# Banded attention with 512-key and 640-key query blocks in alternation

## The reference, cut to what matters

```python
def sliding_window_attention(q, k, v, k_c, v_c, sink):
    '''Banded attention |i - j| <= SWA_RADIUS plus all context keys, with sink logits.'''
    nb = seq // Q_BLOCK                       # 4 blocks of 128 queries
    band = np.abs(qoff[:, None] - koff[None, :]) <= SWA_RADIUS
    ...
    def block_step(j):
        start = j * Q_BLOCK
        ...
        kpos = start - SWA_RADIUS + jnp.arange(span)
        valid = band & ((kpos >= 0) & (kpos < seq))[None, :]
        mask = jnp.concatenate([valid, ctx_ok], axis=-1)
        return attend(q_j, jnp.concatenate([k_j, k_c], axis=1), jnp.concatenate([v_j, v_c], axis=1),
                      mask=mask, sink=sink)
```

## Time and profile before

| what | us |
|---|---|
| median of three runs | 3674.49 |
| lowest and highest of the three | 3672.79, 3674.63 |
| the profiled execution, its own time | 3677.19 |
| its span in the trace | 3675.4 |
| the banded attention, from its first scores to its last values | 3124.3 to 3263.2, 138.9 |

### The profile page before, as it was taken

One profiled execution on the slowest core, in us unless ns is written; L12 is line 12 of the kernel. 1 busy time (PEld: TensorE's weight loads), 2 busy tenths in 40 slices (PEclk: granted clock), 3 DMA queues, 4 the chain that ended last, 5 costly groups with the idle time before them and its releaser, 6 DMA issues.

```text
span 3675.4 us, 58161 instructions
## 1 busy us (share of the span) xinstructions
PE 3601.3 (98%) x19482; PEld 2948.1 (80%) x19482; DVE 2135.1 (58%) x3272; ACT 1832.1 (50%) x3517; POOL 1844.7 (50%) x1583
## 2 busy tenths in 40 slices
PE   9999999999999989999999999999999999999999
PEld 7877788888888767888888887788888997678887
DVE  6576742788635766427886664742236977743234
ACT  4565544434445664444444645843445653754343
POOL 4424673565544245735565763265564135145553
PEclk9999999999999999999999999999999999999999
DMA  4211241465322112414653422132223542012222
GB/s 145 94 64 41 75 144 63 154 192 190 105 92 86 64 41 84 145 59 163 192 188 109 143 89 90 59 104 97 97 92 119 175 166 81 2 58 86 97 97 86
DMA packets 106912, 388.58 MB, mean 106 GB/s; under 512 B 11856, under 2 KB 11984, under 8 KB 106320
## 3 DMA queue, kind: packets, MB, share of 16 engines
q1 hardware_dynamic: 87840, 318.81, 26.2%
q10 hardware_dynamic: 16416, 57.62, 4.7%
q0 software_dynamic: 2448, 9.43, 0.7%
HBM read 383.71 MB, written 2.10 MB: 105 GB/s over the span
## 4 chain that ended last, share of the span: by engine, by line
PE 74%; issue 13%; POOL 7%; DVE 4%; ACT 1%; ACTq 0%; POOLq 0%; DVEq 0%
PE ps L713 18%; PE ps L715 18%; PE ps L714 18%; POOL arena_parts L656 4%; PE ps L1207 2%; PE ps L2507 2%; PE ps L2530 2%; POOL arena_parts L666 1%; PE ps L2497 1%; PE ps L1226 1%; PE ps L1215 1%; POOL lines L440 1%; PE ps L1185 1%; PE ps L889 1%; PE ps L970 1%
## 5 line engine op out<-in xcount | busy, mean ns | idle before, releaser
L714 PE MATMUL ps<-arena_parts 128*128 128x512 f32 (+1 forms) x3148 | 1170.7, 372 | 0.0
L656 POOL TENSOR_TENSOR arena_parts<-ring,arena_parts 128x512 fp32r<-128x512 f32 x508 | 674.6, 1328 | 811.2 <-ACT arena_parts L633 809.1
L666 POOL TENSOR_TENSOR arena_parts<-ring,arena_parts 128x512 fp32r<-128x512 f32 x508 | 688.9, 1356 | 301.1 <-ACT arena_parts L642 300.0
L713 PE MATMUL ps<-h_parts,arena_parts 128*128 128x512 f32 x2080 | 814.5, 392 | 1.3 <-DVE arena_parts L563 1.2
L715 PE MATMUL ps<-h_parts,arena_parts 128*128 128x512 f32 x2080 | 809.4, 389 | 0.0
L1864 DVE SCALAR_TENSOR_TENSOR conv<-ps,cols,conv 128x511 f32<-128x511 f32 (+3 forms) x536 | 377.3, 705 | 536.9 <-ACT conv L1879 388.1
L714 PEld LDWEIGHTS ps<-arena_parts 128*128 128x128 f32 x3148 | 594.0, 189 | 104.4 <-issue 2.4
L633 ACT ACTIVATE arena_parts<-ring 128x512 fp32r<-128x512 f32 x574 | 360.2, 628 | 602.8 <-PE ps L715 570.8
L642 ACT ACTIVATE arena_parts<-ring 128x512 fp32r<-128x512 f32 x574 | 359.9, 627 | 596.2 <-PE ps L715 553.9
L713 PEld LDWEIGHTS ps<-h_parts,arena_parts 128*128 128x128 f32 x2080 | 390.5, 188 | 85.9 <-issue 3.3
L715 PEld LDWEIGHTS ps<-h_parts,arena_parts 128*128 128x128 f32 x2080 | 390.4, 188 | 81.0
(11 more groups left out here) (394 smaller groups left out, 6392.6 us busy)
## 6 DMA issues: line engine op xcount, KB each, us to landing
ring<-in_stream SPq DMA_DIRECT2D x606, 512.0 KB, 3.3
ctx<-in_mod ACTq DMA_DIRECT2D x48, 512.0 KB, 3.5
sq<-in_mod ACTq DMA_DIRECT2D x48, 512.0 KB, 3.4
sq<-in_bias POOLq DMA_DIRECT2D x8, 512.0 KB, 4.7
conv<-in_bias POOLq DMA_DIRECT2D x8, 512.0 KB, 4.5
arena<-in_mem ACTq DMA_DIRECT2D x2, 1024.0 KB, 5.7
out_y<-x ACTq DMA_DIRECT2D x8, 256.0 KB, 2.7
x<-in_x SPq DMA_DIRECT2D x4, 256.0 KB, 4.8
```

The source lines that it names most:

```text
L656: eng.tensor_tensor(side_of(lin, i, c, 0, to), side_of(lin, i, c, 0, raw), side_of(lin, i, c, 0, top), ALU.subtract)\
L666: eng.tensor_tensor(side_of(lin, i, c, 1, to), side_of(lin, i, c, 1, raw), side_of(lin, i, c, 1, top), ALU.subtract)\
L713: pe.matmul(out, w_h, x_h, start=start, stop=False)
L714: pe.matmul(out, w_h, x_r, start=False, stop=False)
```

## The change

The loop over a pair's four query blocks goes first, second, fourth, third. Nothing else is edited: masks, keys, values and the target columns of each block are worked out from its number b as before.

```diff
             for p in range(PAIRS):
                 kv = p // 2
-                for b in range(QB):
+                for b in (0, 1, 3, 2):
                     lo_b, hi_b = max(b - 1, 0), min(b + 2, QB)
```

## The result

| what | before | changed |
|---|---|---|
| median of the runs of one comparison, 20 each, us | 3672.67 | 3678.57 |
| lowest and highest | 3669.03, 3678.68 | 3675.51, 3684.31 |
| span of the profiled execution | 3675.4 | 3680.3 |
| the banded attention, first scores to last values | 3124.33 to 3263.20, 138.87 | 3125.56 to 3268.24, 142.68 |

The changed kernel takes 1.0015 times as long, interval 1.0009 to 1.0021, which is 5.5 us more, 3.3 to 7.7. That is inside the 0.2% that I had set as no change, and the time of 3678.57 is inside the range. The trace puts 3.8 us of it into the stage. Of the 4.9 us between the two spans, 1.2 had come up before the stage began, where the two kernels are the same; spans of one and the same kernel differ by more than that (3680.3 here, 3674.2 in the second trace of the changed kernel), so I compare stages and not spans.

A forecast was written before the change was run, and what follows sets the result against it. TensorE, busy 98% of the span, was taken as the bound, so only its waits could move the time. Steady pairs, first pair and last pair: 0.9 + 0.3 + 1.2 = +2.4 us, median 3676.9, range 3672.5 to 3681.0.

The forecast's parts named there:

- The wait at the boundary goes: Between pairs, the wait behind VectorE's L2189 would be hidden by an S at unit 5: 0.52 us a pair removed.
- 0.15 at each D even with VectorE free: At each D, TensorE's cover of 4.44 us against a chain of 4.59: a new wait of 0.15, 0.30 a pair.
- VectorE late at the pair's first D: Mask 0.37 late, wait 0.52 to 0.54; waits 0.70 a pair against 0.52, so +0.9 over five steady pairs.
- First pair, +0.3: In the stage's first pair, small waits of 0.4 in all before and 0.7 after: +0.3, bounds 0 and +0.6.
- Last pair, +1.2: A 2.0 us wait ahead of turn(46), with L666 between L2582 and L2806; waits 3.9 against 2.7: +1.2.
- The clock: Rival: in the last pair the clock falls behind the new 2.0 us wait, losing 3 us: +5.4, 3679.9; chance 0.27.
- the harmless 2.02: Idle time of 2.02 us at 364.94 in the profile before, behind which the granted clock stayed at 1.00, 2.4 GHz.

The follow-up runs named there:

- the faster order: Order second, first, third, fourth in all pairs, against the kernel before, with L2184 and L2189 where they were: 3671.71 us, ratio 0.9987.

## Why the prediction was right, and where its sizes were off

1. *The wait at the boundary goes.* Right: the units there wait no more, and no row of the second D shows L2189 ahead of it.
2. *0.15 at each D even with VectorE free.* Right: 0.17 in the trace, and 0.165 by itself in the kernel with remainder and key copies moved. Plain addition of TensorE's work on one side and of the chain on the other was good to 0.02 us.
3. *VectorE late at the pair's first D.* The size is right, 0.34 late and a wait of 0.52 against 0.37 and 0.52 to 0.54, and so is the route, L2184 stuck behind a sink's exponential. But the step was told as if L2189 were the whole obstacle. With L2189 gone, 0.30 of the wait came back by another way, GpSimd's key copies. The same sink exponential was close to being late at both block ends.
4. *First pair, +0.3.* Measured 0.39 (16.99 and 16.60). Steps 3 and 4 together were to give 1.2 over the first seven pairs and gave 1.5. The sum had counted five middle pairs, where six periods lie between the second pair's first scores and the last pair's: they took 96.22 against 95.15, 1.07 more, 6 x 0.16 and a little for a pause of VectorE told of below.
5. *Last pair, +1.2.* The mechanism is right to the instruction: stall 1.85 against 2.0, turn(46) 6.85 behind its scores against 7.0. The last pair came to +2.35, and less the 1.6 that the clock's fall cost, to +0.8, so this term was too large by 0.4.
6. *The clock.* This is the step that failed in the forecast: I gave it 0.27 and it happened in both traces of the changed kernel. I had argued from the length of the idle time, 1.85 to 2.0, near to the harmless 2.02. And that row was harmless only in the one trace that I had: at the same instruction in the changed kernel's first trace the idle time was 1.77 (363.04) and the clock read 0.63 and 0.52 behind it. In the last pair the fall cost 1.6 us and not the 3 of that rival, because the clock was back sooner than at the start, whose windows I had taken the 3 from (they add up to 3.4).

The stage: forecast +2.4, found +3.8, of which 1.6 are the clock and 2.2 all the rest. So the waits were forecast well, with two misses of size in steps 4 and 5 that partly cancel, and the fall of the clock was left out. The forecast of 3676.9 is 1.7 below 3678.57, but that owes something to luck: the kernel before ran at a median of 3672.67 in this comparison, 1.8 under the 3674.49 that I had added to. Told as a difference, +2.4 lies below the interval of the ratio, 3.3 to 7.7, which leaves out just what the clock rival held; the range had been drawn past that rival, and so it holds the time.

What the ratio's interval holds beyond the stage's 3.8 I can't place for certain: behind the stage the two traces agree to 0.1 us, and the repeat gave 1.0009. The clock also falls in many places outside the stage, and not in the same ones each time. Added up over windows of 2 us, from the start of the span to 10 us before its end, it was short of 23.8 us in the first trace of the changed kernel (span 3680.3), 18.8 in the second (3674.2) and 22.1 in that of before (3675.4). That is 5.0 between two traces of one kernel, whose spans differ by 6.1, as much as the whole effect. This is why only stages are compared here.

What stays open is when the clock falls and for how long. It fell behind 1.85 in both traces, behind 1.31 close upon 0.27 in all four that begin with the second block, and behind 2.50 in eight traces of nine; it stayed up behind 2.50 in one, behind 1.34, 1.18 and 0.62. At the place of the earlier trace rows it stayed up behind 2.02, 1.83 and 1.82 in three traces and fell behind 1.77 and 1.80 in two; in the other eight the idle time was 1.4 to 1.6 and the clock stayed up. The length of the idle time doesn't decide it, and no run here separates what does.

For the faster order, alone in its kernel, the marks can be the last block's scores, unit 5 of a pair in both. Up to those of the second pair it took 27.36 us and before 29.24, less clock lost included; from there to those of the seventh 78.26 and 79.44; from there to the end of the stage 28.71 and 30.25. So 1.9 of its 4.5 us are the start, 1.2 the middle and 1.5 the end, where the brackets are 0.41 and 0.41 and were 0.57 and 1.21. The end I didn't run by itself.

## What to carry to other kernels

Alternating long and short units evens the load of the engine that does them, but each long unit still needs as much of other work behind it as its own chain is long: add up both sides for every one of them, as step 2 does, before counting a removed wait as a gain. When blocks are put in another order, look at where they *end*: two ends side by side queue their end chains on the slowest small engine, and whatever bulk work stands between them there (L666, L2799, L2801) is paid by everyone. And where a change puts a new idle time of 1.3 us or more before the matrix engine, put the clock's fall into the forecast with about an even chance, not into a rival: of the 30 such idle times told of here 16 were followed by a fall, and what decides it stays open.

## What the runs showed of the chip that I had not expected

*The clock can fall behind an idle time of 1.85 us*; and behind one and the same idle time of 2.50 it fell in eight traces and not in a ninth. What the clock was short of was 3.4 us in each of the eight, and 1.7 in each of the six other falls of the stage, nothing between. In time the longer one cost 2.6 to 2.7 and the shorter one in the last pair 1.6.

*VectorE pauses once in the stage with nothing to wait for.* One pair of the changed kernel took 16.34 instead of 15.99, and one of before 16.09 instead of 15.83. The pause stands ahead of the 147th VectorE instruction behind the stage's first scores, whichever that is (before, then changed):

```profile
3205.17 0.29 DVE L2600 COPY inv_row<-ps 128x128 f32<-128x128 f32 x1 [0.27 <-issue]
```

```profile
3207.70 0.17 DVE L2576 RECIPROCAL inv<-sum 128x2 f32<-128x2 f32 x1 [0.27 <-issue]
```

"Issue" is a pause with nothing to wait for in the profile. Ten of the thirteen traces have such a row, 0.27 to 0.29, all ahead of the 147th instruction. In the four with the changed order and L2189 in its old place a pair is 0.34 to 0.35 longer, in the two with the old order and the old place 0.26 to 0.28; in the other four it leaves no mark on the period. Why it stands there no run shows.

*The remainder L2189 beside a GpSimd instruction.* It took 1.76 beside L666 before; in the last pair of the changed kernel, with L666 over 0.94 ahead of it, its row reads 0.69 (3255.80). In five of the thirteen traces it starts while a 128x512 subtraction of GpSimd (L666 or L656) is running, 0.06 to 0.78 behind its start: it then takes 1.04 to 1.76 and ends 0.54 to 0.55 behind GpSimd's end each time. In the kernel with the remainder moved both start at once, and there it is GpSimd's that is longer, 1.82 instead of 1.28:

```profile
3245.04 1.82 POOL L656 TENSOR_TENSOR arena_parts<-ring,arena_parts 128x512 fp32r<-128x512 f32 x1
3245.04 0.68 DVE L2189 TENSOR_TENSOR h_parts<-h,arena_parts 128x512 fp32r<-128x512 f32 x1
```
